# Two transformer layers on one core: order of columns, layout of split weights and operand addresses

## Time and profile before

| | us |
|---|---|
| median of 3 runs | 1994.62 (1994.3 to 1995.16) |
| profiled execution, first to last instruction (span) | 1992.6 |
| granted TensorE clock over the span | 0.999 of full |

### The profile page before, as it was taken

The page is one execution under the profiler, slowest core; times in us unless marked ns, Lnnn a source line. Parts: engine busy times, 40 slices in busy tenths (PEclk is TensorE's granted clock), DMA queues, the critical chain, the costliest instruction groups (busy, mean ns, idle before and its releaser), DMA issues.

```text
span 1992.6 us, 33224 instructions
## 1 busy us (share of the span) xinstructions
PE 1979.7 (99%) x11726; PEld 1746.3 (88%) x11726; DVE 1418.9 (71%) x1969; ACT 992.0 (50%) x1180; POOL 143.9 (7%) x157
## 2 busy tenths in 40 slices
PE   9999999999999999999999999999999999999998
PEld 8998888888888888888899899888888888888886
DVE  6856788877887786554567668788778877865444
ACT  6556445555545554343455654554555555534433
POOL 1112220000000000110120004100000000011000
PEclk9999999999999999999999999999999999999999
DMA  8566655555555555556575445655555556676654
GB/s 299 177 196 161 196 188 189 177 200 191 189 175 193 193 194 192 190 176 205 191 237 179 132 136 179 197 184 178 190 193 195 189 183 196 207 235 213 200 188 137
DMA packets 106870, 379.67 MB, mean 191 GB/s; under 512 B 12107, under 2 KB 12684, under 8 KB 106668
## 3 DMA queue, kind: packets, MB, share of 16 engines
q1 hardware_dynamic: 102332, 362.22, 54.7%
q0 software_dynamic: 4176, 16.07, 3.2%
q10 hardware_dynamic: 288, 0.33, 0.1%
HBM read 368.09 MB, written 10.49 MB: 190 GB/s over the span
## 4 chain that ended last, share of the span: by engine, by line
PE 96%; DVE 2%; DMA 1%; SPq 0%; ACT 0%; issue 0%; ACTq 0%
PE ps L429 46%; PE ps L432 24%; PE ps L823 4%; PE ps L822 4%; PE ps L821 4%; PE ps L723 2%; PE ps L725 2%; PE ps L724 2%; DMA raw<-weights 1%; DVE w_lo L1172 1%; PE ps L761 1%; PE ps L784 1%; PE ps L459 1%; PE ps L460 1%; PE ps L458 1%; PE ps L772 1%
## 5 line engine op out<-in xcount | busy, mean ns | idle before, releaser
L1172 DVE TENSOR_TENSOR w_lo<-raw,w_hi 128x1024 fp32r<-128x1024 f32 (+1 forms) x678 | 824.9, 1230 | 498.5 <-ACT w_hi L861 477.2
L861 ACT ACTIVATE w_hi<-raw 128x1024 fp32r<-128x1024 f32 (+1 forms) x678 | 710.4, 1054 | 778.4 <-PE ps L432 454.9
L429 PE MATMUL ps<-op_in,w_hi 128*128 128x512 f32 x2992 | 1026.4, 391 | 1.7 <-DVE w_lo L1205 0.9
L432 PE MATMUL ps<-op_in,w_lo 128*128 128x256 f32 x2992 | 812.3, 282 | 0.0
L429 PEld LDWEIGHTS ps<-op_in,w_hi 128*128 128x128 f32 x2992 | 548.9, 188 | 106.1 <-issue 1.3
L432 PEld LDWEIGHTS ps<-op_in,w_lo 128*128 128x128 f32 x2992 | 564.8, 189 | 15.7
L429 PE MATMUL ps<-op_ffn,w_hi 128*128 128x512 f32 x704 | 243.1, 390 | 0.0
L432 PE MATMUL ps<-op_ffn,w_lo 128*128 128x256 f32 x704 | 195.8, 282 | 0.0
L429 PEld LDWEIGHTS ps<-op_ffn,w_hi 128*128 128x128 f32 x704 | 131.1, 188 | 26.5
L821 PE MATMUL ps<-w_hi,op_ffn 128*128 128x512 f32 x352 | 139.5, 396 | 0.0
L822 PE MATMUL ps<-w_lo,op_ffn 128*128 128x512 f32 x352 | 139.5, 396 | 0.0
(11 more groups left out here) (218 smaller groups left out, 2052.4 us busy)
## 6 DMA issues: line engine op xcount, KB each, us to landing
raw<-weights SPq DMA_DIRECT2D x662, 512.0 KB, 4.1
raw<-weights SPq DMA_DIRECT2D x16, 384.0 KB, 3.1
bias_rows<-brow POOLq DMA_DIRECT2D x1, 6144.0 KB, 36.1
win_bias<-bias_rows POOLq DMA_DIRECT2D x4, 1024.0 KB, 8.4
h<-xt SPq DMA_DIRECT2D x8, 256.0 KB, 7.2
raw<-weights SPq DMA_DIRECT2D x8, 256.0 KB, 6.2
x_tok<-x_rows SPq DMA_DIRECT2D x4, 512.0 KB, 8.7
h_rows<-h_blocks POOLq DMA_DIRECT2D x16, 128.0 KB, 5.5
```

Of the source, the lines that this page charges most:

```text
L429: return mm(ps[:, bank, 0:2 * T], whi, op, start=start, stop=stop)
L432: return mm(ps[:, bank, 0:T], wlo, op[:, 0, :], start=False, stop=False)
L861: f(w_hi[s][:, 0:cols], raw[s][:, 0:cols], ACT.Copy).then_inc(hi_ready, 1)
L1172: v.tensor_tensor(w_lo[s][:, 0:cols], raw[s][:, 0:cols], w_hi[s][:, 0:cols].bitcast(F32), ALU.subtract).then_inc(lo_ready, 1)
```

## The change

1. A slot's w_hi and w_lo become one tensor `ring[s]` of 2048 words. Where its weights will be stationary, word 2c is the hi and word 2c+1 the lo part of column c; where they will be the moving operand (`rows_hi`, `rows_lo`), hi and lo stand in two contiguous halves, as before. ScalarE's and VectorE's `split` writes whichever layout the chunk n needs; where that switches inside a hardware loop, the last turn is written out.
2. `back(a, size)` is an access pattern over the same words from last to first. All products with stationary weights read their moving operand through it and write PSUM through it. Products with moving weights are left as they are.
3. The operands start at a multiple of 256 bytes, and `par` shrinks from 896 to 832 words.

```diff
+def back(a, size):
+    return bass.AP(a.tensor, a.offset + size - 1, [list(a.ap[0]), [-1, size]])
...
-    w_hi = [new(f"w_hi{s}", [P, CH], F32R) for s in range(SLOTS)]
-    w_lo = [new(f"w_lo{s}", [P, CH], F32R) for s in range(SLOTS)]
+    ring = [new(f"ring{s}", [P, 2 * CH], F32R) for s in range(SLOTS)]
+    w_hi = [r[:, :].rearrange("p (c two) -> p c two", two=2)[:, :, 0] for r in ring]
+    w_lo = [r[:, :].rearrange("p (c two) -> p c two", two=2)[:, :, 1] for r in ring]
+    rows_hi = [r[:, 0:CH] for r in ring]
+    rows_lo = [r[:, CH:2 * CH] for r in ring]
...
-    par = new("par", [P, 7 * P])
+    par = new("par", [P, PC_END])
...
-    top[0] = (top[0] + 127) // 128 * 128 + 32
+    top[0] = (top[0] + 255) // 256 * 256
...
                 def high():
-                    return mm(ps[:, bank, 0:2 * T], whi, op, start=start, stop=stop)
+                    return mm(back(ps[:, bank, 0:2 * T], 2 * T), whi, back(op[:, 0, :], 2 * T), start=start, stop=stop)
 
                 def low():
-                    return mm(ps[:, bank, 0:T], wlo, op[:, 0, :], start=False, stop=False)
+                    return mm(back(ps[:, bank, 0:T], T), wlo, back(op[:, 0, :], T), start=False, stop=False)
...
-                        mm(o, hi, wcols(w_hi[s], k), start=first and k == 0, stop=False)
+                        mm(o, hi, wcols(rows_hi[s], k), start=first and k == 0, stop=False)
...
-                    o = ps[:, bank + j // 2, j % 2 * T:(j % 2 + 1) * T]
+                    o = back(ps[:, bank + j // 2, j % 2 * T:(j % 2 + 1) * T], T)
...
-                        mm(o, w_hi[s][:, w], op[:, kt0 + k, 0, :], start=first and k == 0 and j % 2 == 0, stop=False)
+                        x_hi, x_lo = back(op[:, kt0 + k, 0, :], T), back(op[:, kt0 + k, 1, :], T)
+                        mm(o, w_hi[s][:, w], x_hi, start=first and k == 0 and j % 2 == 0, stop=False)
...
-                f(w_hi[s][:, 0:cols], raw[s][:, 0:cols], ACT.Copy).then_inc(hi_ready, 1)
+                f(hi[s][:, 0:cols], raw[s][:, 0:cols], ACT.Copy).then_inc(hi_ready, 1)
...
-                v.tensor_tensor(w_lo[s][:, 0:cols], raw[s][:, 0:cols], w_hi[s][:, 0:cols].bitcast(F32),
+                v.tensor_tensor(halves[1][s][:, 0:cols], raw[s][:, 0:cols], halves[0][s][:, 0:cols].bitcast(F32),
                                 ALU.subtract).then_inc(lo_ready, 1)
...
-                done.loop(0, FFN_TURNS, 19, body)
+                done.loop(0, FFN_TURNS - layer, 19, body)
+                if layer == 1:
+                    body(None, FFN_TURNS - 1)
```

More of the change, by code:

```diff
@@ L437, in feature_tile, with w_chunk @@
                 return low()
-            def w_chunk(n, op, kt0, first, last, b0, tiles=(0, 1, 2, 3)):
+            def w_chunk(n, op, kt0, first, last, b0, tiles=(0, 1, 2, 3), halves=(w_hi, w_lo)):
                 s = n.mod(SLOTS)
+                whi, wlo = halves[0][s], halves[1][s]
                 pe.wait_ge(lo_ready, (n + 1).v)
@@ L851, in _, with split @@
             f = nc.scalar.activation
-            def split(n, cols=CH):
+            def split(n, cols=CH, hi=w_hi):
                 if n.i is None and n.c >= CHUNKS:
@@ L954, in q_group @@
                 for c in range(2):
-                    split(k.times(2) + (ph.c0 + AHEAD_2 + c), cols)
+                    split(k.times(2) + (ph.c0 + AHEAD_2 + c), cols, w_hi if cols < CH else rows_hi)
                     if c == 0 and k.c == 5:
@@ L974, in kv_group @@
                     for c in range(2):
-                        split(k.times(2) + (ph.c0 + AHEAD_2 + c))
-            repeat(act, 0, 3, lambda i: [kv_group(Lin(k, 2, i)) for k in range(2)])
-            kv_group(Lin(6))
+                        split(k.times(2) + (ph.c0 + AHEAD_2 + c), hi=rows_hi if k.c < 5 else w_hi)
+            repeat(act, 0, 2, lambda i: [kv_group(Lin(k, 2, i)) for k in range(2)])
+            for k in range(4, 7):
+                kv_group(Lin(k))
             kv_group(Lin(7), False)
@@ L1033, in body @@
                     for j in range(2 * per):
-                        split(Lin(ph.c0 + AHEAD + j + 2 * per * t, 2 * per, i))
+                        next_rows = rows_next and t == 1 and j >= 2 * per - AHEAD
+                        split(Lin(ph.c0 + AHEAD + j + 2 * per * t, 2 * per, i), hi=rows_hi if next_rows else w_hi)
                         gi, at = divmod(j, per)
@@ L1164, in _, with split @@
             done = Steps(dve, dve_done)
-            def split(n, cols=CH):
+            def split(n, cols=CH, halves=(w_hi, w_lo)):
                 if n.i is None and n.c >= CHUNKS:
@@ L1356, in q_group @@
                         rope_finish(Lin(8), 3, xr[:, 1, :], q_rope[:, UNITS_A - 1:UNITS_A, :])
-                    split(k.times(2) + (ph.c0 + AHEAD_2 + c), cols)
+                    split(k.times(2) + (ph.c0 + AHEAD_2 + c), cols, (w_hi, w_lo) if cols < CH else (rows_hi, rows_lo))
             for k in range(UNITS_A):
@@ L1375, in kv_group @@
                     for c in range(2):
-                        split(k.times(2) + (ph.c0 + AHEAD_2 + c))
-            repeat(dve, 0, 3, lambda i: [kv_group(Lin(k, 2, i)) for k in range(2)])
-            kv_group(Lin(6))
+                        split(k.times(2) + (ph.c0 + AHEAD_2 + c), halves=(rows_hi, rows_lo) if k.c < 5 else (w_hi, w_lo))
+            repeat(dve, 0, 2, lambda i: [kv_group(Lin(k, 2, i)) for k in range(2)])
+            for k in range(4, 7):
+                kv_group(Lin(k))
             kv_group(Lin(7), False)
@@ L1466, in body @@
                     for j in range(2 * per):
-                        split(Lin(ph.c0 + AHEAD + j + 2 * per * t, 2 * per, i))
+                        next_rows = rows_next and t == 1 and j >= 2 * per - AHEAD
+                        split(Lin(ph.c0 + AHEAD + j + 2 * per * t, 2 * per, i),
+                              halves=(rows_hi, rows_lo) if next_rows else (w_hi, w_lo))
                         gi, at = divmod(j, per)
```

82 lines of the change are left out of this document (45 added, 37 removed).

## The result

The changed kernel takes 2007.34 us (median of 3, 2006.8 to 2007.6) against 1994.62 us: ratio 1.0063, interval 1.0043 to 1.0083. It is slower by 12.7 us where some 65 us less, 1930 us, was forecast. Its profiled execution has a span of 2004.9 us, 12.3 more than before.

A forecast was written before the change was run, and what follows sets the result against it. TensorE's product pace was taken as the bound. Gains of 58.0 us (pairs) and 7.2 us (narrow products), together 65, off the 1992.6 us span gave 1927.6; with 2.0 us from span to median, 1930 us, range 1890 to 2030.

The forecast's parts named there:

- The bound: Whole kernel: TensorE, busy 1979.7 of 1992.6 us, sets the time by its products' pace, unless another engine falls behind.
- So I credit collisions with 9 ns in each, 18 ns per pair; the other 4 ns stay: Wide and narrow products of the 4144 pairs: load and stream reads colliding cause 18 of the 21.7 ns above the floor.
- the 14 ns: Gain taken per pair, midway between one product's stall gone (about 10) and both (18); 4144 pairs give 58.0 us.
- The mechanism: Stationary loads beside streams: alternating words equalise their speeds, and descending order may keep their distance constant, avoiding repeated meetings.
- The 1440 narrow ones: 256-column products on the operand's split halves (L723 to L725, L545 to L547): 5 of 7.5 ns each gained, 7.2 us.
- Weights as the moving operand: 1056 products of the last stage, 288 in the value parts: only partner addresses move; 19 us either way, taken as 0.
- PSUM from last to first: Descending PSUM writes of the products with stationary weights: same banks and count, so no cost taken.
- rival D: Turned-round products: descending access at plain fp32 pace, 0.21 us per 256 columns; 1308 us more, about 3300 us; 4%.
- Alternating words for the splits: ScalarE and VectorE splits, about 678 times: step of two words taken as costing nothing; VectorE has 0.57 us free per split.
- Rival C: Stationary loads: slower at an 8-byte step, or equal-speed reads lock into always meeting; 2015 to 2555 us; 14%.
- mild form: Stationary loads of the pairs: alternating layout costs only 5 ns more per pair, giving 2015 us; within the 14%.
- The half-rate form: Stationary loads at half rate take 218 ns, a pair 447 ns; 560 us more, 2555 us; within the 14%.

The follow-up runs named there:

- e11: Kernel before with each w_lo load of the pairs' narrow products cut to 64 of 128 columns; 1994.6 us, ratio 1.0.
- e13: Kernel before with w_lo loads and most w_hi loads of the pairs cut to 64 of 128 columns; 1992.98 us, ratio 0.9994.
- e3: Changed kernel with ascending order and separate halves restored, so only operand addresses (and written-out loop turns) differ from before; 2005.75 us, ratio 1.0054.
- e9: Old form (ascending, halves apart), weight slots at 224, operands at 0, 160, 128 and 224 by stage; 1991.44 us, ratio 0.9985.
- e16: Kernel before with w_chunk's stationary loads reading 32 bytes further on, splits writing where they did; 2016.89 us, ratio 1.0116.
- e8: Old form (ascending, halves apart) with operands at 128, 192, 224 and, in the last projection, 128, modulo 256; 2008.94 us.
- e17: Ascending, halves-apart kernel with operands at multiples of 256, w_chunk's loads reading every second word, splits writing contiguous halves; 2022.33 us, ratio 1.0143.
- e2: Changed kernel with only the order taken back: ascending operand and PSUM, words still alternating, operands at multiples of 256; 2024.27 us, ratio 1.0148.

## Why the prediction was wrong, step by step

- *The bound* was right: the products' pace sets the time, no other engine took over, and the difference is counted products times nanoseconds, within 0.6 us of the span's.
- *The failed step* is "So I credit collisions with 9 ns in each, 18 ns per pair; the other 4 ns stay", and with it the 14 ns taken of them. I took nearly all that a pair needs above 215.8 + 109.2 ns as collisions with the load that the change could remove, because the transposes reach 109 ns. But the transposes are plain float32 with 128 columns, and their loads are recorded at 140 ns where those of the products have 188, so their spacing need not be what the fast format can reach:

```profile
L772 PEld LDWEIGHTS ps<-ident,probs_b 128*128 128x128 f32 x96 | 10.9, 140 | 0.0
```

Halving both loads (e11, e13) moved a pair by 0.1 ns, and no address, order or spacing tried gave a pair below 347.0. The term was 58 us of gain and measured 17.2 us of loss: 4.0 of the 4.1 ns per pair are the address (e3), the rest the new form at that address.
- *The mechanism* was half right. The load's address relative to the stream's does set the pace (e9, e16), and at address 0 descending order and alternating words together cost 6.3 ns less than their single costs added. That equal speeds are the reason is not shown: no run changes the speed alone, and at address 160 the same two parts give the slowest pair of all, 356.7 ns. I had not looked at where the kernel before stood: at distance 32, one of the two where its form is fastest. I wrote that I could not see whether the kept distance was a good one, and then credited a gain all the same. The change left a 347 ns address for a form that is at best 351.
- *The 1440 narrow ones*: 7.2 us less forecast, 1.4 more measured; same step.
- *Weights as the moving operand*: taken as 0 within 19 us either way (19.2 ns x 1056 is 20.3); -5.7 us, inside its bounds.
- *PSUM from last to first*: taken as nothing, and rival D is out. Order of reading and of writing were never separated here, so the 2.4 ns of descending order alone at address 0 may belong to either.
- *Alternating words for the splits*: right in effect. VectorE kept its 1.22 us. Of the two rules of the Trainium skill weighed there, the trace disagrees with "Vector Engine (DVE) Microarchitecture Reference" (section 5.2: 1.7 ns and more per column without adjacent pairs) for a step of two words, and agrees for VectorE with the 16-byte lines of "SBUF — State Buffer". ScalarE's 1059 ns became 1183, which by that second rule should not be; it was hidden in its slack, which was (489 - 255.7)/176 = 1.3 us per chunk and not 1.2.
- *Rival C* came nearest in time, with its mild form of 5 ns per pair and 2015 us against 4.1 ns and 2007.34. I gave it 14% and slower 28% in all, the rest of that to cases that did not happen. Its remark that the distance is a matter of luck in addresses is what e3 to e8 bear out. But 5 ns was a size picked without a row, so that it comes so near is luck, and the sign I gave for C, longer spacings at L432, did not come: the narrow product went from 118.3 to 118.5 ns and the wide one took the loss. A load at a step of 8 bytes does cost where the order is ascending (e17, 4.2 ns per pair). The half-rate form did not come: the record of such a load is 6 to 9 ns longer, not 109.

## What to carry to other kernels

Where TensorE is 99% busy, count products in a stretch of fixed length: an effect of 1% on the pace is plain there as 12 products of 1155 (e3). The distance, modulo 256 bytes, between what is loaded and what is streamed moved a pair of this kernel by up to 1.8% within one form and a product of its last projection by 3.4%. It is cheap to sweep, several values in one run, if each stage has its own operand. Before crediting a change with removing a loss, shorten the supposed cause once; and compare a new form at its best address with the old form at its best.

## What was not expected of the hardware

- The pace depends on distance and not on either address: 347.1, 353.2 and 347.2 ns were repeated within 0.2 ns after both had moved by 96 bytes (e9).
- The smallest spacings found in the fast format were 226.7 ns for 512 columns (213.3 of stream) and 116.7 for 256 (106.7); no distance, direction or step came below, nor did half-length loads at the one distance tried. In the trace of before, some 770 wide products during which no DMA packet was in flight took 228.5 ns and some 1300 with 15 or more in flight 228.6, so transfers are not the cause. What these last 6 to 9% are stays open.
- A ScalarE copy that writes every second float32 takes 12% longer in the changed kernel (1183 ns against 1059 for 1024 columns; 1152 in e2). Where the same kernel writes contiguous words, in the last projection, it is back at 1059. A VectorE subtraction that reads one such operand and writes one takes no longer (1225 against 1223).
